# Two heads at a time: preparation of a pair spread over 13 planning rounds in place of 17

## The chip, the cores and the metric

The kernel runs on one core of one Trainium2 chip. The core has five engines that this text names: TensorE (PE, with its weight loads shown apart as PEld), VectorE (DVE), ScalarE (ACT), GpSimd (POOL) and SyncE (SP), which here only starts transfers. Each engine works through its own list of instructions in order and waits on semaphores for the others. The metric is the time of one execution on the device in microseconds, lower is better.

## The reference, cut to what matters

The whole program is three transformer-like blocks over 256 latent tokens and 256 context tokens of width 1024. Only one part of the first block is touched: the recurrent mixer of eight heads, four pairs of heads `p` = 0 to 3, each run in two directions `d` (forward, backward).

```
kk = (k * k_k);  kk = kk / max(sqrt(sum(kk * kk)), 1e-12)
w_raw = w0 + tanh(wl) @ w2[d];   iclr = sigmoid(a0 + al @ a2[d])
decay = exp(-exp(-softplus(-w_raw) - 0.5))
k_dir = k * (1 + (iclr - 1) * k_a)
state = state * w_t + (state @ -kk_t) (kk_t * a_t) + v_t k_t      # 512 steps, per head and direction
y_t   = state @ r_t
```

The steps over time are computed 64 at a time: within a chunk of 64 steps a triangular system is solved with small matrix products, and the chunks are chained afterwards.

## The kernel before, in words

**Stages.** After the projections and the window attention of the first layer (the stage that ends with `step("end", "even")`) comes the stage of the units. A unit is one pair of heads, one direction and one half of the tokens (four chunks of 64), so there are 16 units. `unit` (line 923) gives out its work in 13 rounds: the Gram products (`unit grams`), five levels of the triangular inverse (`unit lt` and `unit tlt`, ten rounds), the solve, and the outputs with the states.

**Preparation.** Before a unit can run, its pair and direction must be prepared. `prepare(p)` (line 811) gives out: squares of the keys, their sums, a clamp and a root, four reciprocals of 128 columns each (`prep recip`, DVE, line 2389) with the product into `kk`, the turned values (`prep v`), and then for each direction two low-rank products (`prep lora`, PE, lines 1915 and 1917, sigmoids on ACT), a scan along time (`prep decay`, DVE, line 2397), exponentials and the gain of the keys (`prep exps`, DVE line 2410, ACT), and products with them (`prep scale`, `prep last`). For pairs 1 to 3 POOL makes these products: in `prep exps` lines 1601 and 1604 or 1606, in `prep scale` lines 1611, 1613 and 1615, in `prep last` lines 1620 and 1622. The last of them, line 1622, tells PE that the direction is prepared; `unit grams` waits for it (line 1852). For pair 0 DVE makes them. POOL also masks each unit's Gram products (lines 3130, 3133, 3136) and makes the mask of one level for each of three `unit lt` steps (line 3136).

**The plan.** The order of the work on every engine comes from one list, `plan`, written by Python generators. `run(...)` asks each generator for one piece in turn; one pass over all of them is called a round here. A `yield` ends what a generator gives out in this round. Each engine later goes through the whole plan in its order and takes out its own part. So a round has no time of its own: it only fixes in what order an engine meets the pieces. In the stage of the units a round asks, in this order: four lanes (each takes the next unit of `work` when it is done with its last, lane n starts 4n rounds later), `preparing`, `chaining` (the chain over the chunks, lines 1933 and 1939 on PE, lines 2448 and 2455 on DVE, and the group norm at the end of a pair with its own reciprocals, line 2466) and `conditions` (32 slices of the modulation product, 16 matmuls of line 1687 each, one in every second round). A lane whose next unit isn't prepared in the plan gives out nothing in that round. The preparation of pair 1 follows on pair 0's; that of pair 2 waits until all units of pair 0 are given out, that of pair 3 for pair 1.

Pair 0 starts earlier, in the stage before, where `begun()` (line 860) asks `prepare(0)` for 11 pieces between projections and attention.

Matmuls of the units all have line 1832 (a helper), copies out of PSUM on ACT line 2727.

Of the kernel before, what the change touches and what calls it, by code (L numbers as in the profile page):

```python
def program(nc, I, C, out):
# [192 lines left out]
    def step(*a):  # L194
        plan.append(a)
# [10 lines left out]
    def take(*key):  # L206
        assert idle, "no bank"
        b, before = idle.pop(0)
        assert key not in uses, key
        uses[key] = Use(b, before)  # L210

    def give(*key):
        u = uses[key]
        idle.append((u.b, u.empty))
# [596 lines left out]
    def prepare(p):  # L811
        step("prep squares", p)
        yield
        take("kk sums", p)
        step("prep sums", p)
        yield
        give("kk sums", p)
        step("prep norm", p)
        yield
        for i in range(4):  # L820
            step("prep recip", p, i)
            if i % 2:
                yield
        for q in range(2):
            take("v turned", p, q)
            step("prep v", p, q)
            give("v turned", p, q)
        yield
        for d in range(2):
            if p or not d:  # L830
                prep_lora(p, d)
                yield
            step("prep decay", p, d)
            yield
            step("prep exps", p, d)
            yield
            step("prep scale", p, d)
            yield
            if not p and not d:
                prep_lora(p, 1)  # L840
                yield
            step("prep last", p, d)
            prepared.add((p, d))
            yield
        step("prep rk", p)
        yield
        take("bonus", p)
        step("prep bonus", p)
        give("bonus", p)

    def prep_lora(p, d):
        take("w", p, d)
        take("a", p, d)
        step("prep lora", p, d)
        give("w", p, d)
        give("a", p, d)

    now = prepare(0)

    def begun():  # L860
        while not projected >= {4, 8, 12, 13}:
            yield
        for _ in range(11):
            next(now)
            yield

    run(a_proj(), b_rotate(), begun(), slowed(modulation(0, 8, 16)))
    step("end", "even")
    top[0] = m_b
# [108 lines left out]
    def preparing(first):  # L978
        yield from first
        for p in range(1, 4):  # L980
            while p > 1 and not all((p - 2, d, h) in finished for d in range(2) for h in range(2)):
                yield
            yield from prepare(p)
# [2367 lines left out]
```

How the kernel before makes its waits and increments, by code:

```python
        def wait_ge(self, sem, value):  # L62
            return self
# [23 lines left out]
        def wait_ge(self, *points):  # L87
            if isinstance(self.e, Stub):
                return
            far = {}
            for p in points:
                if p is not None and p.value > max(self.seen.get(p.of, 0), far.get(p.of, 0)):
                    far[p.of] = p.value
                assert p is None or p.of is not None
            for c, v in far.items():
                self.e.wait_ge(c.h, v)
                self.seen[c] = v
# [1500 lines left out]
    def keys(e, q, p, d):  # L1598
        ka, k = KA[p % 2][d], pA[:, 4 + p, :]
        q.wait_ge(q.last(), at("ka gain", p, d))
        e.tensor_tensor(ka, ka, k, MUL).then_inc(*q.tick())
        q.wait_ge(q.last(), *([at("bonus", p - 1)] if p else []))
        if d == 0:
            e.tensor_copy(kb, ka).then_inc(*q.tick())
        else:
            e.tensor_tensor(kb, kb, ka, ADD).then_inc(*q.tick())
# [1 line left out]
    def scaled(e, q, p, d):  # L1608
        be, ka = BE[p % 2][d], KA[p % 2][d]
        q.wait_ge(q.last(), at("kk", p))
        e.tensor_tensor(be, be, kk, MUL).then_inc(*q.tick())
        q.wait_ge(q.last(), at("falls", p, d))
        e.tensor_tensor(be, be, sg, MUL).then_inc(*q.tick())
        q.wait_ge(q.last())
        e.tensor_tensor(ka, ka, sg, MUL).then_inc(*q.tick(at("scaled", p, d)))
# [1 line left out]
    def rotated(e, q, p, d):  # L1617
        ar = AR[p % 2][d]
        q.wait_ge(q.last(), at("exps", p, d), *(() if p else stage("even")))
        e.tensor_tensor(ar[:, 0, :], cu, kk, MUL).then_inc(*q.tick())
```

## Time and profile before

| | us |
|---|---|
| median of 3 runs | 1977.13 (1973.98 to 1978.09) |
| the profiled execution's own time | 1983.05 |
| its span, first to last instruction | 1981.2 |
| PE busy in the span | 1815.8 |
| stage of the units in the profile | about 245 to 616 |
| PE busy in that stretch | 333.76 of 371.00 |

The span leaves out what lies around the program's own instructions (1983.05 - 1981.2 = 1.85 us). Busy time of PE is the union of its matmuls; weight loads are apart. The mean granted TensorE clock of the execution is 0.958 of full speed.

### The profile page before, as it was taken

The numbers are of one execution on the slowest core, as the hardware profiler recorded it, in microseconds if no ns is written. First come the engines' busy times: TensorE is split into PE (matmuls) and PEld (weight loads), VectorE is DVE, ScalarE is ACT, GpSimd is POOL, SyncE is SP. The second block draws the span as 40 slices with busy tenths as digits, with TensorE's granted clock in tenths as the row PEclk, the third lists the DMA queues.
The fourth block names the chain that finished last, engine by engine and source line by source line (L and its number), as shares of the span: only waits on it lengthen the run. The fifth ranks groups of instructions, "written<-read, shape, count | busy, mean of one in ns | idle before, by whom it ended". The sixth has DMA issues, their size and how long they took to land.

```text
span 1981.2 us, 39345 instructions
## 1 busy us (share of the span) xinstructions
PE 1815.8 (92%) x16690; PEld 1502.1 (76%) x16690; DVE 1103.9 (56%) x1626; ACT 871.7 (44%) x1374; POOL 224.0 (11%) x222
## 2 busy tenths in 40 slices
PE   4999888988898899999998998899989999889997
PEld 2867677877687688888887766798877677769985
DVE  4357654565455744324435866565455475757863
ACT  4136544353332544213325266465332366536643
POOL 0000036334353000000001100000000000000210
PEclk8999989999998999999999999899989999989998
DMA  8341152232222323232324411365545523435542
GB/s 285 112 153 61 55 169 88 94 103 88 87 88 69 124 64 106 85 106 86 107 85 97 148 44 43 108 191 182 190 128 168 191 86 103 150 117 180 191 159 96
DMA packets 201372, 237.13 MB, mean 120 GB/s; under 512 B 14347, under 2 KB 158573, under 8 KB 201197
## 3 DMA queue, kind: packets, MB, share of 16 engines
q1 hardware_dynamic: 196267, 227.52, 35.8%
q10 hardware_dynamic: 4930, 7.11, 1.1%
q8 instruction: 131, 2.15, 0.5%
q14 instruction: 44, 0.36, 0.1%
HBM read 233.56 MB, written 1.05 MB: 118 GB/s over the span
## 4 chain that ended last, share of the span: by engine, by line
PE 74%; DVE 12%; ACT 7%; issue 2%; POOL 2%; DMA 2%; ACTq 0%; SPq 0%; DVEq 0%; POOLq 0%
PE bank L1636 17%; PE bank L1637 17%; PE bank L1638 17%; PE bank L1832 9%; DVE window L2139 3%; ACT window L2727 3%; PE bank L1687 2%; DMA arena<-in_w_ada 2%; PE bank L1820 2%; PE bank L1799 2%; PE bank L1811 1%; PE bank L1839 1%; PE bank L1803 1%; DVE arena L2209 1%; DVE arena L2466 1%
## 5 line engine op out<-in xcount | busy, mean ns | idle before, releaser
L1638 PE MATMUL bank<-window 128*128 128x512 f32 (+1 forms) x1980 | 687.5, 347 | 0.0
L1637 PE MATMUL bank<-window 128*128 128x512 f32 (+1 forms) x1904 | 676.6, 355 | 0.0
L1636 PE MATMUL bank<-window 128*128 128x512 f32 (+1 forms) x1732 | 626.2, 362 | 41.4 <-DVE window L2139 16.5
L1638 PEld LDWEIGHTS bank<-window 128*128 128x128 f32 x1980 | 384.9, 194 | 46.3
L1636 PEld LDWEIGHTS bank<-window 128*128 128x128 f32 x1732 | 338.3, 195 | 101.1 <-DVE window L2139 21.9
L1637 PEld LDWEIGHTS bank<-window 128*128 128x128 f32 x1904 | 371.7, 195 | 46.4 <-issue 0.5
L2139 DVE TENSOR_TENSOR window<-arena,window 128x2048 fp32r<-128x2048 f32 (+1 forms) x132 | 296.6, 2247 | 192.3 <-ACT window L2727 190.7
L2727 ACT ACTIVATE window<-arena 128x2048 fp32r<-128x2048 f32 (+2 forms) x252 | 311.0, 1234 | 183.4 <-DMA arena<-in_w_ff 50.9
L2727 ACT ACTIVATE arena<-bank 128x256 f32<-128x256 f32 (+1 forms) x266 | 115.9, 436 | 352.1 <-PE bank L1638 130.3
L1832 PEld LDWEIGHTS bank<-arena 64*64 64x64 f32 x5888 | 205.0, 139 | 33.8 <-issue 10.3
L1832 PE MATMUL bank<-arena 64*64 64x64 f32 (+1 forms) x5888 | 218.1, 230 | 12.1 <-ACT arena L2727 4.0
L3136 POOL TENSOR_TENSOR arena<-arena 128x256 f32<-128x256 f32 x80 | 68.4, 855 | 331.6 <-DMA arena<-t_id 198.5
L2948 ACT ACTIVATE arena<-bank 128x512 f32<-128x512 f32 (+1 forms) x64 | 31.5, 492 | 146.6 <-PE bank L1638 145.3
L2139 DVE TENSOR_TENSOR window<-arena,window_extra 128x2048 fp32r<-128x2048 f32 (+1 forms) x32 | 71.2, 2226 | 36.7 <-ACT window_extra L2727 36.4
L2356 DVE TENSOR_TENSOR arena<-arena,bank 128x512 f32<-128x512 f32 (+1 forms) x80 | 50.8, 635 | 64.5 <-PE bank L1832 60.7
L1636 PE MATMUL bank<-window,window_extra 128*128 128x256 f32 (+1 forms) x248 | 78.8, 318 | 2.5 <-POOL window L3147 2.5
L2850 ACT ACTIVATE arena<-bank,arena 128x512 f32<-128x512 f32 (+3 forms) x112 | 58.6, 523 | 50.7 <-DVE arena L2300 32.7
L1687 PE MATMUL bank<-arena 128*32 128x256 f32 x768 | 58.7, 424 | 23.0 <-DMA arena<-in_w_ada 20.6
L3178 POOL TENSOR_TENSOR arena<-arena 128x256 f32<-128x256 f32 x22 | 20.0, 911 | 527.6 <-DVE arena L2682 527.0
L1637 PE MATMUL bank<-window,window_extra 128*128 128x256 f32 (+1 forms) x248 | 78.5, 317 | 0.0
L2489 DVE TENSOR_TENSOR arena<-arena 128x512 f32<-128x512 f32 (+1 forms) x48 | 28.9, 603 | 86.2 <-ACT arena L2948 85.6
L1636 PE MATMUL bank<-window_extra,window 128*128 128x512 f32 (+1 forms) x172 | 67.3, 392 | 3.0 <-DVE window L2139 3.0
(298 smaller groups left out, 2028.3 us busy)
## 6 DMA issues: line engine op xcount, KB each, us to landing
arena<-in_w_ff SPq DMA_DIRECT2D x64, 1024.0 KB, 5.4
arena<-in_w_ada SPq DMA_DIRECT2D x48, 1024.0 KB, 6.0
arena<-in_w_in SPq DMA_DIRECT2D x23, 1024.0 KB, 5.1
arena<-in_w_ffn_up SPq DMA_DIRECT2D x22, 1024.0 KB, 5.1
arena<-in_w_ffn_down SPq DMA_DIRECT2D x10, 1024.0 KB, 5.1
arena<-in_w_in_even SPq DMA_DIRECT2D x9, 1024.0 KB, 5.5
arena<-in_w_out SPq DMA_DIRECT2D x8, 1024.0 KB, 5.0
arena<-in_w_in_odd SPq DMA_DIRECT2D x8, 1024.0 KB, 5.5
```

The source lines that it names most:

```text
L1636: e.matmul(o, rr(l[0]), rr(r[0]), start=start, stop=False)
L1637: e.matmul(o, rr(l[0]), rr(r[1]), start=False, stop=False)
L1638: return e.matmul(o, rr(l[1]), rr(r[0]), start=False, stop=stop)
L1687: t = e.matmul(u.b[q:q + 32, 0:256], SV[:, k, 6 - 2 * g:38 - 2 * g], w.v[:, k, :], start=g == 0 and k < 4, stop=g == 3 and k >= 4)
L1799: t = e.matmul(b if it["ns"] > 1 else b[:, 0], it["q"][h0:h1], k, start=True, stop=not it["masks"])
L1820: t = e.matmul(u.b[h0:h1, oc:oc + 128], vs[h], a.PT[i % a.NT][h][0:kw, x * 128:x * 128 + 128], start=it["begin"] and x == 0, stop=it["end" ...
L1832: t = e.matmul(o[h0:h1, c], l[i][h0:h1, c], r[i][h0:h1, c], start=i == 0, stop=i == len(l) - 1)
L2139: e.tensor_tensor(rr(raw), raw, rr(w.high, F32), SUB).then_inc(*ve.tick(w.ready))
L2356: e.tensor_tensor(w, w, x, SUB).then_inc(*ve.tick(b.empty, at("w", *u)))
L2727: return e.activation(o, i, ACT.Copy, **k)
L2850: e.activation(a.P[i % a.NP][h][:, s * n:s * n + n], u.b[:, s * n:s * n + n], ACT.Exp, bias=low[:, x:x + 1], accum_out=total[:, x:x + 1]). ...
L3136: return e.tensor_tensor(z.L[l % 2], z.G[:, :, 0], lvl[:, 1 - d, l:l + 1, :].to_broadcast([128, NCH, 64]), MUL)
```

## The change

The four reciprocals are given out in one round together with the turned values, and after them, in place of two rounds before them. For pairs 1 to 3 the round between `prep scale` and `prep last` goes. `prepare(p)` then has 13 rounds for pairs 1 to 3 and 15 for pair 0, where it had 17 for each. `begun()` asks for 9 pieces in place of 11, so that the pieces of pair 0 in the stage before end at the same step. No instruction is added or removed.

```diff
@@ prepare(p)
         step("prep norm", p)
         yield
-        for i in range(4):
-            step("prep recip", p, i)
-            if i % 2:
-                yield
         for q in range(2):
             take("v turned", p, q)
             step("prep v", p, q)
             give("v turned", p, q)
+        for i in range(4):
+            step("prep recip", p, i)
         yield
...
             step("prep exps", p, d)
             yield
             step("prep scale", p, d)
-            yield
+            if not p:
+                yield
             if not p and not d:
                 prep_lora(p, 1)
                 yield
@@ begun()
-        for _ in range(11):
+        for _ in range(9):
             next(now)
             yield
```

## Rows read from the trace of the kernel before

**Rows 1.** The page, part 1: busy us of each engine, share of the span, instructions.

```profile
PE 1815.8 (92%) x16690; PEld 1502.1 (76%) x16690; DVE 1103.9 (56%) x1626; ACT 871.7 (44%) x1374; POOL 224.0 (11%) x222
```

**Rows 2.** Busy time by stretch, units' stage and before; columns in the first row.

```profile
core 0: us, PE busy (x) PEld busy (x) DVE busy (x) ACT busy (x) POOL busy (x), PEclk, DMA share, GB/s
245.00:616.00 371.00, 333.76 (x8190) 285.13 (x8186) 203.83 (x368) 146.25 (x292) 154.22 (x154) 0.94 0.30 99
...
150.00:245.00 95.00, 88.81 (x626) 62.63 (x626) 70.09 (x163) 58.53 (x128) 0.00 (x0) 0.97 0.15 45
```

**Rows 3.** PE's waits, 245 to 616: waiter, releaser, us in total, times, longest.

```profile
PE bank L1832 <- POOL extra L1622: 12.6, 3, 5.7
PE bank L1933 <- DVE extra L2448: 5.8, 2, 3.6
PE bank L1832 <- ACT arena L2727: 4.0, 4, 1.8
PE bank L1832 <- POOL arena L1622: 3.3, 1, 3.3
...
PE bank L1832 <- DVE arena L2356: 1.8, 1, 1.8
```

**Rows 4.** Line 1687 alone: durations ns (min/median/max), first and last start us.

```profile
L1687 PE MATMUL bank<-arena x512: 377/379/635, 251.9 to 587.6; 128*32 128x256 f32 x171
```

**Rows 5.** POOL in order of time, 300 to 317: start, us, idle before.

```profile
300.09 1.96 POOL L3136 TENSOR_TENSOR arena<-arena 128x256 f32<-128x256 f32 x2 [8.75 <-ACT arena L2727]
302.13 1.52 POOL L3130 TENSOR_TENSOR arena<-arena 128x256 f32<-128x256 f32 x1
303.73 1.59 POOL L3133 TENSOR_TENSOR arena<-arena 128x512 f32<-128x512 f32 x1
305.40 1.93 POOL L3136 TENSOR_TENSOR arena<-arena 128x256 f32<-128x256 f32 x2
307.41 1.28 POOL L1601 TENSOR_TENSOR arena<-arena 128x512 f32<-128x512 f32 x1
...
313.48 0.72 POOL L3136 TENSOR_TENSOR arena<-arena 128x256 f32<-128x256 f32 x1
...
315.62 1.26 POOL L1622 TENSOR_TENSOR extra<-arena 128x512 f32<-128x512 f32 x1
```

**Rows 6.** PE in order of time around the first unit of pair 1.

```profile
300.73 1.07 PE L1687 MATMUL bank<-arena 128*32 128x256 f32 x16
...
305.19 1.61 PE L1832 MATMUL bank<-arena 64*64 64x64 f32 x48 [1.84 <-ACT arena L2727]
...
316.94 2.83 PE L1832 MATMUL bank<-extra 64*64 64x64 f32 x48 [5.24 <-POOL extra L1622]
```

**Rows 7.** Busy time after that stall, columns as in Rows 2.

```profile
315.00:322.00 7.00, 5.06 (x74) 5.06 (x76) 1.39 (x2) 1.19 (x3) 4.10 (x5) 0.52 0.00 0
```

**Rows 8.** POOL for pair 2, first direction: first and last piece.

```profile
415.57 1.09 POOL L1601 TENSOR_TENSOR arena<-arena 128x512 f32<-128x512 f32 x1 [12.66 <-DVE arena L2410]
...
422.27 1.59 POOL L1622 TENSOR_TENSOR arena<-arena 128x512 f32<-128x512 f32 x1
```

**Rows 9.** PE around the first unit of pair 2.

```profile
426.29 0.45 PE L1933 MATMUL bank<-extra,arena 64*64 64x64 f32 x8 [3.56 <-DVE extra L2448]
...
428.21 3.99 PE L1832 MATMUL bank<-arena 64*64 64x64 f32 x74
```

**Rows 10.** POOL for pair 3, second direction: first and last piece.

```profile
547.51 1.27 POOL L1601 TENSOR_TENSOR arena<-arena 128x512 f32<-128x512 f32 x1 [0.66 <-DVE arena L2410]
...
557.22 1.26 POOL L1622 TENSOR_TENSOR extra<-arena 128x512 f32<-128x512 f32 x1
```

**Rows 11.** The reciprocals of the preparation, grouped: busy us, mean ns.

```profile
L2389 DVE RECIPROCAL arena<-arena 128x128 f32<-128x128 f32 x12 | 11.4, 953 | 0.4
```

**Rows 12.** PE where pair 1's second direction is first used.

```profile
348.53 1.57 PE L1832 MATMUL bank<-extra 64*64 64x64 f32 x48
```

**Rows 13.** POOL's last piece for it.

```profile
346.17 1.28 POOL L1622 TENSOR_TENSOR extra<-arena 128x512 f32<-128x512 f32 x1
```

## The prediction

> **What bounds the kernel now.** Start with the busy times of the page [rows 1]: PE works 1815.8 of 1981.2 us, so only its idle time and its clock can give or cost much. The change touches the stage of the units, so the next view is the busy time of that stretch [rows 2]: PE is busy 333.76 of 371.00 us, POOL 154.22, DVE 203.83. 37.24 us of PE's idle time lie here, and the stage can win no more than that, plus what the clock loses with it (mean 0.94). Who ends that idle time stands in PE's waits [rows 3]. The largest share is POOL line 1622, the last product of a preparation: 12.6 us in 3 waits and 3.3 us in one, 15.9 in all. So in four of the six cases of pairs 1 to 3 PE stood at `unit grams` and waited until the direction was prepared. The rest is small: 5.8 us for the chain's DVE step, 4.0 for ACT copies, 1.8 for DVE. The stage is a full PE with holes, and the largest holes are the preparation that comes too late for its first unit.
>
> **What a round is worth.** The 32 slices of line 1687 are in every second round, the first in round 1, and start at 251.9 and about 587 us [rows 4]: 335.5 / 62 = 5.4 us for a round, idle time included. The stage has 70 rounds before (counted below), so PE's work is 333.76 / 70 = 4.8 us in a round.
>
> **Counting the rounds.** From the generators, with round 1 the first of the stage. Before, the pieces `prep last` of (pair, direction) (1,0), (1,1), (2,0), (2,1), (3,0), (3,1) are in rounds 16, 21, 35, 40, 52, 57, and in each case a free lane takes the first unit in the next round. After, they are in rounds 13, 17, 32, 36, 45, 49, and again a lane is waiting or comes free for the next round each time. The last unit ends in round 64 in place of 70. The same work of PE then lies in 64 rounds, 333.76 / 64 = 5.2 us in each. No instruction goes, so PE's busy time doesn't fall: fewer rounds save nothing by themselves. What changes is how much other work PE finds between a step of the preparation and its use.
>
> **The removed round of cover.** POOL's part begins with the gain of the keys in `prep exps` and ends with line 1622. Before, `exps`, `scale`, `last` and the first unit are in rounds R, R+1, R+2, R+3; after, in R, R+1, R+2 with `scale` and `last` together. PE has the rest of round R and one full round less to do meanwhile. Two full rounds of 4.8 us become one of 5.2: 9.6 - 5.2 = 4.4 us of cover go, six times.
>
> POOL's part itself takes 423.86 - 415.57 = 8.3 us when nothing comes between [rows 8] and 558.48 - 547.51 = 11.0 us with level masks between [rows 10]; the six lie in this range. Level masks that the vanished round put between `scale` and `last` (0.72 us for one [rows 5]) now come later; I take 3 us off for them over the six.
>
> Now the six, with the wait or the slack of before. (1,0): 5.24 us wait [rows 6]. (1,1): PE starts at 348.53 and line 1622 ended at 347.45 [rows 12, 13], a slack of 1.1. (2,0): line 1622 ends at 423.86, PE starts the unit at 428.21 [rows 8, 9], slack 4.35. (2,1): 3.3 wait [rows 3]. (3,0) and (3,1): the longest, 5.7, and the remaining 12.6 - 5.24 - 5.7 = 1.7 [rows 3, 6]. With 4.4 us less cover: 9.6, 3.3, 0.05, 7.7, 10.1, 6.1, together 36.9; less the 3 us, 34. Before 15.9. **Term 1: +18 us.**
>
> **A check on (1,0), worked out on its own.** Before, PE's round 13 ends with line 1687 at 300.73 + 1.0 = 301.7 [rows 6], and rounds 14 to 16 cover the preparation until the wait. After, the unit is in round 14, so PE stands at 301.7. POOL starts the Gram masks of the unit of round 13 at 300.09, as ACT lets it, and ends them at 303.73 + 1.59 = 305.3 [rows 5]. The key gains, now a round earlier, fit into its 8.75 us of idle time before that. Then come the five products of `scale` and `last` at 1.34 us each: 305.3 + 6.7 = 312.0. PE waits 10.3 us, against 5.24 + 1.84 before [rows 6]. The mean rule gave 9.6, so it isn't too dark here.
>
> **What is won.** Preparation and lanes move against the chain and the norm. The waits that aren't line 1622's are 5.8 + 4.0 + 1.8 = 11.6 us in PE's list [rows 3]. The ACT wait of 1.84 at 305 falls inside a longer wait; 3.56 at 426 stands where PE waits for a chain step on DVE [rows 9], which in the new plan follows a wait in which DVE catches up; reciprocals of norm and preparation of pair 3 no longer share a round. I take 7 of the 11.6. Bounds: 0 and 11.6. **Term 2: -7 us.**
>
> **Reciprocals together.** Twelve at 0.953 us in the stage [rows 11]: four in one round hold DVE 3.8 us and the product into `kk` follows. A lane's DVE result is used in the lane's next round, 5.2 us on, so the burst hides; only where two lanes stack behind it would it show. Three times at most 3.8 us as the upper bound, 0 as the lower, since no instruction goes. I take 0. The same for pair 0, whose pieces come up to two rounds earlier beside the attention: PE is busy 88.81 of 95.00 us there [rows 2], DVE 70.09. At best it wins 2 of the idle 6.2, at worst one burst of 3.8 shows; I take 0. The stage's transfers are the 32 slices of the modulation, two rounds apart as before, and nothing on SP moves past them.
>
> **Clock.** In the stretch after the wait of 5.24 the granted clock is 0.52 on average over 7 us [rows 7], the lower of the levels 1.2 and 2.4 GHz nearly throughout. PE was partly idle in it, so of 7 us at half speed up to 5.06 us of busy time went at half rate, some 2.5 us lost. Waits that now become long (two more by the list above: (2,1) and (3,1) over 6 us, (1,1) not) can each bring a stretch like it, and those at (1,0) and (3,0) have theirs already. I take 2 us in all, bounds 0 and 5. **Term 3: +2 us.**
> The Trainium skill, TensorE: Matmul & The Clock Gate, section "HAM oscillation — how this bites in real kernels", says that waits between bursts of matmuls throttle the array again and that the loss is half of the time spent throttled. By that rule, an estimate from the page, the stretch of 7 us would cost 3.5 us where the row gives 2.5 and two new ones 7 us in place of 2; the trace shows the throttled stretch after the wait, but not that each long wait brings one.
>
> **Sum.** 18 - 7 + 2 = +13 us. The profiled execution of before took 1983.05 us, 1981.2 in its span, so its like would take 1996; it is 5.9 us over the median of the runs, 1977.13. On the median: 1990.
>
> **Rivals.**
> *Faster: denser rounds cover what the removed round did.* The lanes idle less (rounds 14 to 16 and 18 to 21 before), so between `exps` and the first unit PE may find as much work as before; the reciprocals and pieces of the chain no longer meet on DVE. Then waits on line 1622 stay at 15.9 and most of the 11.6 of the others go, say 9: 1977 - 9 = 1968. For it speaks that slack of 4.35 was unused at (2,0); against it the count at (1,0), where POOL sets the end at 312.0 whatever PE has. It decides from the point where a full round holds over 9 us of PE's work; the mean is 5.2.
> *Nothing: POOL's end moves with the rounds.* The gain of keys stands behind the lanes' DVE steps of its round, and if each is reached 4 us sooner in PE's time because the round before is lighter, terms 1 and 2 cancel: 1977, within 4 us.
> *Heavier: the whole loss shows.* Each case loses a full 5.2 us and the chain's waits stay: 15.9 + 31.2 - 5.45 of slack = 41.7, so +26, nothing won, clock +5: 2008, or 1977 + 28 = 2005 if POOL's 3 us come off.
> *The change doesn't do what it says:* pair 0 still has 15 rounds; that changes nothing in the stage of the units, since its second direction is prepared in round 4 in both plans. It is no case of its own.
>
> **How the numbers follow.** Forecast 0.56, faster 0.20, nothing 0.14, heavier 0.10. A difference of 0.2%, about 4 us, is what a measurement can tell from no change. The forecast's own range is 1982 to 2001. The range down to the faster rival and up to most of the heavier one is 1967 to 2004. Of the forecast some 0.02 lies inside 4 us: slower 0.64, same 0.16, faster 0.20.
>
> **What would show it.** PE's waits between 245 and 616 should have line 1622 at 28 to 40 us in place of 15.9, the one at (1,0) near 10 us and ending at about 312; PE's idle time in the stage near 48 in place of 37; its busy time within 5 us of 334; one more or two more stretches at the lower clock. The wait at DVE line 2448 should be smaller. It is wrong if line 1622's waits stay under 20 us, if busy time moves by more than idle time, or if the difference lies outside the stage.

## The result, and the profile after

The changed kernel takes 1985.01 us (median of 5 runs, 1982.62 to 1987.52) against 1978.07 for the kernel before: a ratio of 1.0034, 95% interval 1.0019 to 1.0049, which is 3.8 to 9.7 us, 6.7 in the middle. The forecast was +13 on the median, 1990, in a range of 1967 to 2004. The direction held and the size came out at half. The two profiled executions differ by less (1983.05 and 1985.01 us), because that of before lies 5 us above the median of its kernel's runs; so here the stages are compared, not the spans.

One line is missing from the changed file ahead of all engines' code, so line 1622 of before is 1621 after, 1687 is 1686, and so on.

First the busy time by stretch (columns as in [rows 2]): from PE's first instruction whose place the change moves to pair 0's first unit, and from there to the last unit. Before:

```profile
145.20:244.60 99.40, 90.39 (x626) 63.52 (x624) 73.62 (x165) 60.39 (x131) 0.00 (x0) 0.96 0.19 59
244.60:614.90 370.30, 333.57 (x8178) 285.07 (x8180) 203.29 (x368) 146.25 (x292) 154.22 (x154) 0.94 0.30 99
```

After:

```profile
144.75:250.20 105.45, 90.78 (x626) 63.78 (x622) 73.61 (x165) 62.83 (x133) 0.00 (x0) 0.95 0.17 55
250.20:618.10 367.90, 330.08 (x8176) 281.81 (x8176) 198.63 (x367) 147.32 (x293) 149.35 (x154) 0.94 0.31 100
```

The stage of the units, where the prediction put the loss, became 2.4 us shorter (370.30 to 367.90). The stretch ahead of it, where the prediction put nothing, became 6.05 us longer (99.40 to 105.45) with the same busy time: PE's idle time there is 9.0 before and 14.7 after.

A second profile of the kernel before (1977.33 us) shows how far one program's profiles differ:

```profile
144.90:243.10 98.20, 89.39 (x624) 62.75 (x624) 72.90 (x163) 60.43 (x131) 0.00 (x0) 0.98 0.19 59
243.10:612.70 369.60, 332.99 (x8150) 285.41 (x8152) 204.27 (x369) 146.00 (x292) 154.03 (x154) 0.95 0.31 99
```

About a microsecond in each stretch. So the +6 ahead of the units is clear of that, and the -2.4 in the units is barely so. A kernel with the change for pairs 1 to 3 alone (below) has the same order in the units and doesn't have the -2.4:

```profile
244.40:615.40 371.00, 331.82 (x8176) 281.89 (x8176) 198.62 (x367) 147.49 (x293) 148.75 (x154) 0.94 0.30 99
```

So no gain of the stage is shown.

PE's waits after, 252 to 640 us (columns as in [rows 3]):

```profile
PE bank L1831 <- POOL extra L1621: 12.1, 4, 9.2
PE bank L1831 <- POOL arena L1621: 10.2, 2, 7.6
...
PE bank L1831 <- ACT arena L2726: 3.2, 4, 1.4
PE bank L1949 <- ACT arena L2936: 2.7, 2, 2.3
```

The last product of the preparation now makes PE wait 22.3 us in six waits, where [rows 3] have 15.9 in four. That is +6.4 us where the prediction had +18; which of the two edits brings it is seen only in the experiments. The first of these waits, for pair 1, in POOL's and PE's order of time:

```profile
300.18 1.28 POOL L1600 TENSOR_TENSOR arena<-arena 128x512 f32<-128x512 f32 x1 [1.33 <-DVE arena L2409]
...
307.13 1.96 POOL L3135 TENSOR_TENSOR arena<-arena 128x256 f32<-128x256 f32 x2 [4.99 <-ACT arena L2726]
...
309.97 1.26 POOL L3132 TENSOR_TENSOR arena<-arena 128x512 f32<-128x512 f32 x1
311.31 1.26 POOL L1610 TENSOR_TENSOR extra<-extra,arena 128x512 f32<-128x512 f32 x1
...
316.66 1.26 POOL L1621 TENSOR_TENSOR extra<-arena 128x512 f32<-128x512 f32 x1
```

```profile
307.76 1.07 PE L1686 MATMUL bank<-arena 128*32 128x256 f32 x16
318.07 2.18 PE L1831 MATMUL bank<-extra 64*64 64x64 f32 x36 [9.23 <-POOL extra L1621]
```

This is the check of the prediction come true: the key gain runs before the Gram masks, five products run behind them without a gap, PE stands idle 9.23 us (10.3 forecast). It ends at 318.07; less the 5.60 us by which the units start later (250.20 against 244.60) that is 312.5, where the prediction had 312.0. PE's waits for the chain's DVE step (line 2448 of before, 5.8 us in [rows 3]) are gone in the stage.

What the stretch ahead of the units lost is seen where the order of PE first changes. Line 1838 is the turning of a pair's values on PE. After:

```profile
144.43 0.70 PE L1798 MATMUL bank<-arena 64*128 64x256 f32 x4
145.96 0.68 PE L1838 MATMUL bank<-arena 64*64 64x64 f32 x16 [0.83 <-ACT arena L2726]
149.51 0.68 PE L1838 MATMUL bank<-arena 64*64 64x64 f32 x16 [2.87 <-DVE arena L2270]
152.56 0.79 PE L1635 MATMUL bank<-window 128*128 128x512 f32 x1 [2.37 <-ACT arena L2849]
```

Before, the turning stood behind two more projections:

```profile
148.43 0.79 PE L1636 MATMUL bank<-window 128*128 128x512 f32 x1 [2.82 <-DVE window L2139]
...
175.17 1.25 PE L1839 MATMUL bank<-arena 64*64 64x64 f32 x32
```

6.07 us of idle time in place of 2.82. The releasers are a copy on ACT, DVE's shift of a projection and ACT's exponentials of the attention. The reciprocals, which the prediction had suspected here, run only later (DVE, after):

```profile
154.81 3.92 DVE L2388 RECIPROCAL arena<-arena 128x128 f32<-128x128 f32 x4
```

### The profile page after: what moved, and what is told of

It is laid out like the page before. It is cut to its first block, busy times and chain, and to the rows that moved or that the text cites. A ratio compares the mean times of both kernels' runs of the same rounds, so it can differ in the third digit from the quotient of the medians.

```text
span 1983.2 us, 39337 instructions
## 1 busy us (share of the span) xinstructions
PE 1813.9 (91%) x16690; PEld 1500.7 (76%) x16690; DVE 1100.4 (55%) x1626; ACT 874.7 (44%) x1377; POOL 218.9 (11%) x222
## 4 chain that ended last, share of the span: by engine, by line
PE 74%; DVE 11%; ACT 7%; POOL 3%; issue 2%; DMA 2%; SPq 0%; ACTq 0%; DVEq 0%; POOLq 0%
PE bank L1635 18%; PE bank L1636 17%; PE bank L1637 17%; PE bank L1831 9%; DVE window L2138 3%; ACT window L2726 3%; PE bank L1819 2%; PE bank L1686 2%; DMA arena<-in_w_ada 2%; PE bank L1798 2%; PE bank L1810 1%; PE bank L1838 1%; PE bank L1802 1%; PE bank L2016 1%; DVE arena L2208 1%
## 5 line engine op out<-in xcount | busy, mean ns | idle before, releaser
L1831 PEld LDWEIGHTS bank<-arena 64*64 64x64 f32 x5888 | 203.9, 139 | 38.6 <-issue 11.1
L1831 PE MATMUL bank<-arena 64*64 64x64 f32 (+1 forms) x5888 | 216.5, 229 | 17.9 <-POOL arena L1621 10.2
```

Of the source, the lines that this page charges most:

```text
L1831: t = e.matmul(o[h0:h1, c], l[i][h0:h1, c], r[i][h0:h1, c], start=i == 0, stop=i == len(l) - 1)
```

## The experiments

Every ratio is to the kernel before, measured beside it. Waits on the last product of the preparation (line 1622 of before), by pair and direction, read from PE's order of time in each trace, in us:

| kernel | (1,0) | (1,1) | (2,0) | (2,1) | (3,0) | (3,1) | sum |
|---|---|---|---|---|---|---|---|
| before | 5.2 | 0 | 0 | 3.3 | 5.7 | 1.7 | 16.0 |
| changed | 9.2 | 0.8 | 2.6 | 7.7 | 1.2 | 0.9 | 22.4 |
| reciprocals together | 9.3 | 3.4 | 0 | 1.1 | 1.3 | 6.7 | 21.7 |
| scale and last together | 6.9 | 5.2 | 5.2 | 4.4 | 9.9 | 7.4 | 38.9 |
| by pair | 5.2 | 0 | 0 | 1.1 | 3.0 | 0 | 9.3 |

**Pair 0's part alone.** `prepare(0)` and `begun()` as in the change, pairs 1 to 3 as before.

```diff
+        for i in range(4 if p else 0):
             step("prep recip", p, i)
...
+        for i in range(0 if p else 4):
+            step("prep recip", p, i)
...
-        for _ in range(11):
+        for _ in range(9):
```

> Of the change only pair 0's part: its four reciprocals in one round after the turned values, its pieces two rounds earlier beside the attention; pairs 1 to 3 as before. Theory of the trace (the loss sits in the stage before the units, where PE's idle time rose from 9.0 to 14.7 us in the changed kernel): +5 to +6 us, and the stretch from PE's first different instruction to pair 0's first unit near 105 us in place of 99.4. Rival, the prediction's: pair 0's part costs nothing, 0 us within 2.

1.0038 (1.0026 to 1.0051), +7.5 us. PE's idle time ahead of the units is 14.7 us, the waits of the units stage those of before to 0.1 us. Pair 0's part carries the whole loss; that it costs nothing has fallen.

**Pairs 1 to 3 alone.** Reciprocals together and the round between `scale` and `last` gone for `p` over 0; pair 0 as before.

> Only the part of pairs 1 to 3 (13 rounds each); pair 0 as before with 17. Theory of the trace (the stage of the units became 2 to 3 us shorter although line 1622's waits rose from 16.0 to 22.4 us): -3 to +1 us. Rival, the prediction's: the removed round of cover sets the sum, +7 to +13 us.

1.0001 (0.9990 to 1.0013). The waits are those of the changed kernel. The forecast for these pairs was +13, so its part of the sum fails here. The two halves add up: 7.5 + 0.2 against 6.7 measured, within the intervals.

**Reciprocals together, pairs 1 to 3.**

```diff
-        for i in range(4):
+        for i in range(4 if not p else 0):
...
+        for i in range(0 if not p else 4):
+            step("prep recip", p, i)
```

> For pairs 1 to 3 only the reciprocals in one round (15 rounds for each); scale and last keep their round between them; pair 0 as before. Prediction's view: preparation starts its later pieces two rounds sooner against the lanes, the cover between exps and the first unit stays, so line 1622's waits stay at 16 us or fall, the time falls by 2 to 6 us. Rival: a burst of 3.8 us on DVE delays the lanes: up to +4 us, with new waits of PE on DVE line 2356.

0.9977 (0.9965 to 0.9989), -4.5 us. The waits on the last product rose to 21.7 and yet the time fell, so the first expectation had the time right and the waits wrong. No new wait on DVE shows: line 2356's counterpart holds PE 0.6 us.

This kernel keeps the round between `scale` and `last`, and still has 21.7 us of waits where before has 16.0 and the changed kernel 22.4. So most of the change's +6.4 comes with the reciprocals, not with the removed round. At (1,0) PE has more work in front of the unit than before (10.3 us from the end of the key gain, 5.0 before) and waits longer, because POOL's products now stand behind another unit's masks:

```profile
294.14 1.28 POOL L1603 TENSOR_TENSOR arena<-arena 128x512 f32<-128x512 f32 x1 [1.34 <-DVE arena L2412]
...
301.09 1.96 POOL L3138 TENSOR_TENSOR arena<-arena 128x256 f32<-128x256 f32 x2 [5.00 <-ACT arena L2729]
...
305.28 1.26 POOL L1613 TENSOR_TENSOR extra<-extra,arena 128x512 f32<-128x512 f32 x1
...
312.24 1.26 POOL L1624 TENSOR_TENSOR extra<-arena 128x512 f32<-128x512 f32 x1
```

From the end of the key gain (294.00) to the last product POOL needs 19.5 us, and 10.1 before.

**Scale and last together, pairs 1 to 3.**

```diff
             step("prep scale", p, d)
-            yield
+            if not p:
+                yield
```

> For pairs 1 to 3 only the round between scale and last removed (15 rounds for each); reciprocals and pair 0 as before. Prediction's view: one round of cover less in each of six cases, line 1622's waits rise from 16 to over 28 us, time +8 to +13 us. Rival (the count by average rounds was too coarse; what PE finds in the rounds that are left decides): waits rise by under 8 us and others fall, -2 to +3 us.

1.0110 (1.0093 to 1.0127), +22 us. By itself this edit does what the prediction gave the whole change, and more. Its waits in the trace:

```profile
PE bank L1833 <- POOL extra L1623: 29.3, 4, 9.9
PE bank L1833 <- POOL arena L1623: 9.6, 2, 5.2
```

and the stage of the units:

```profile
243.20:638.00 394.80, 337.43 (x8178) 289.69 (x8180) 200.18 (x368) 146.22 (x292) 151.14 (x154) 0.92 0.29 93
```

38.9 us of waits. Of the 24.5 us by which the stage grew, 20.6 are idle time and 3.9 the same work at a lower mean clock (0.92). The longest wait is that of pair 3's first direction. PE around it:

```profile
524.80 0.61 PE L1695 MATMUL bank<-arena 128*128 128x8 f32 x4
525.35 1.15 PE L1833 MATMUL bank<-arena 64*64 64x64 f32 x32
526.42 1.07 PE L1688 MATMUL bank<-arena 128*32 128x256 f32 x16
537.40 2.83 PE L1833 MATMUL bank<-extra 64*64 64x64 f32 x48 [9.91 <-POOL extra L1623]
```

By the count of the generators two lanes stand still in the last round ahead of the unit, waiting for the preparation of pair 3 (one for each direction), and PE finds 1.1 us of lane work and a slice. In the changed kernel the same round holds a full set:

```profile
508.13 3.89 PE L1831 MATMUL bank<-arena 64*64 64x128 f32 x112
511.85 0.63 PE L1838 MATMUL bank<-arena 64*64 64x64 f32 x16
512.32 2.03 PE L1831 MATMUL bank<-arena 64*64 64x64 f32 x64
514.19 0.63 PE L1838 MATMUL bank<-arena 64*64 64x64 f32 x16
514.75 1.07 PE L1686 MATMUL bank<-arena 128*32 128x256 f32 x16
517.00 1.61 PE L1831 MATMUL bank<-extra 64*64 64x64 f32 x48 [1.18 <-POOL extra L1621]
```

Both this kernel and the one with the reciprocals together end in round 66 by the count of the generators, and they are 26 us apart: the number of rounds says nothing of the time.

**Pair 0: where it costs.** Two kernels, a slip in both: their expectations say that pairs 1 to 3 are as before, but the reciprocals were together in all pairs. Their yardstick is therefore the kernel with the reciprocals together, 0.9977.

The first keeps the early turned values with the burst and puts two rounds behind them; the second puts all of pair 0's preparation two rounds later:

```diff
             step("prep recip", p, i)
         yield
+        if not p:
+            yield
+            yield
```

```diff
     def prepare(p):
+        if not p:
+            yield
+            yield
```

> Pair 0's four reciprocals together in their old round after the root, then two empty rounds, so that its low-rank products and all that follows stand where they stood before; pairs 1 to 3 as before. Theory A (the burst of 3.8 us on DVE, in front of the attention's reductions of that round, makes PE wait): the loss of pair 0's part stays, +4 to +8 us. Theory B (the two rounds by which everything after moves against attention and projections make it): 0 us within 2.

> Pair 0's preparation with four reciprocals together but begun two rounds later, so that its squares and the burst come two rounds later than before and the rest stands where it stood; pairs 1 to 3 as before. Theory A (burst): some loss stays wherever it meets attention, +2 to +8 us. Theory B (position of the later pieces): 0 us within 2.

0.9984 (0.9974 to 0.9995) and 0.9973 (0.9961 to 0.9986). Against the yardstick that is +1.4 us and -0.8, neither told from nothing. The traces are finer: the first has the waits of 0.83, 2.86 and 2.37 us at the turned values again, 11.8 us idle ahead of the units, where the second, whose turned values are back at 175 us, has 9.5, and the yardstick 9.8. So the early round with turned values and burst comes with 2 to 3 us of idle time, the whole preparation begun two rounds later with nothing. No run moved the turned values alone; that it is they and not the burst is read from who waits.

**One round earlier, no burst.**

```diff
-            if i % 2:
+            if i % 2 and (p or i < 3):
...
-        for _ in range(11):
+        for _ in range(10):
```

> Pair 0 with its reciprocals two and two as before, but the turned values in the round of the second two, so that its low-rank products and all later pieces come one round earlier beside the attention; pairs 1 to 3 as before. Theory B (the position of the later pieces costs): +2 to +5 us for one round. Theory A (the burst of four costs): 0 us within 2, since no round has more than two reciprocals.

0.9993 (0.9981 to 1.0005). One round costs nothing, against theory B as it was priced. PE's idle time ahead of the units is even 7.5 us here, 1.5 less than before; but at the first slice of the stage it then waits 4.5 us for its weights (2.8 before). So the loss comes only with two rounds; no run has the two rounds without the burst. Of the 5.7 us of idle time more in the changed kernel, 3.3 are the three waits where the turned values meet the projection (6.07 against 2.82), and 2.4 come later, where all other pieces meet other rounds of the attention: 6.6 us in place of 4.2, on ACT's exponentials, copies and DVE's shift. That the second part comes from the place of the later pieces is read from the trace only, and the 7.5 us of time (5.1 to 10.1) are known less well than the 5.7 us of idle time.

**Last product early, units where they were.**

```diff
             step("prep scale", p, d)
+            if p:
+                step("prep last", p, d)
             yield
...
-            step("prep last", p, d)
+            if not p:
+                step("prep last", p, d)
```

> For pairs 1 to 3 the products of last come with those of scale as in the kernel that lost 21 us, but the direction counts as prepared in the plan one round later, so that every unit and every other piece stands where it stood before. Theory (the loss was cover: the first unit's products stood one round too early in PE's list): -2 to +1 us, waits at 12 to 16 us. Rival (it is the order of POOL's work, five products without a gap in front of the level masks): +5 us or more, with PE waiting for copies and masks.

0.9993 (0.9982 to 1.0004), waits 14.3 us. The same order of POOL's five products as in the kernel that lost 22 us, and nothing lost: what cost was the place of the unit, and of all that moved up with it, in PE's list, not that POOL makes the five products in a row.

**By pair.** Pairs 0 and 1 with 17 rounds, pair 2 with reciprocals together (15), pair 3 with both (13), pairs 1 to 3 each chosen where the table has the smallest waits.

```diff
-        for i in range(4):
+        for i in range(4 if p < 2 else 0):
...
+        for i in range(0 if p < 2 else 4):
+            step("prep recip", p, i)
...
             step("prep scale", p, d)
-            yield
+            if p < 3:
+                yield
```

> Structure by pair: pairs 0 and 1 with 17 rounds as before, pair 2 with reciprocals together (15), pair 3 with reciprocals and scale with last together (13). Theory of counted cover (a wait is what POOL needs after the key gain, 8 to 11 us, less the PE work that the plan puts before the first unit): waits on the last product of the preparation 5 to 9 us in all where they were 16.0, time -6 to -12 us. Rival (the cover of one pair depends on shifts that the other pairs bring, no rule holds): anywhere within 4 us of the kernel with reciprocals together, -4.5.

0.9918 (0.9902 to 0.9935), 1962.51 us, -16 us: more than expected. Its waits and its stage of the units:

```profile
PE bank L1835 <- POOL extra L1625: 8.2, 2, 5.2
PE bank L1690 <- DMA arena<-in_w_ada: 5.1, 1, 5.1
```

```profile
242.60:598.30 355.70, 325.80 (x8178) 277.31 (x8178) 205.66 (x367) 147.50 (x293) 152.47 (x154) 0.97 0.32 103
```

14.6 us shorter than before, 6.8 of them idle time (36.7 to 29.9), 7.8 the same matmuls in less busy time at a mean granted clock of 0.97 in place of 0.94. By the count it ends in round 64, like the changed kernel. The wait of 5.1 us for the weights of the stage's first slice (2.8 before) is nearly as long as the longest one for the preparation; no run went after it. This is the fastest version found.

**By pair, with pair 0 as in the change.**

> The structure by pair of the fastest kernel so far (pair 1 with 17 rounds, pair 2 with 15, pair 3 with 13), and pair 0 as in the change (reciprocals together, all later pieces two rounds earlier beside the attention). If the loss of pair 0's part belongs to the attention stage alone and adds to the rest: +5 to +9 us over the kernel by pair, so -10 to -6 against before, with PE's idle time before pair 0's first unit 5 to 6 us above. Rival (it cost 7.5 us only through what it shifted in the stage of the units): within 2 us of the kernel by pair, -15.

0.9970 (0.9957 to 0.9982), 10 us slower than by pair, just over the +5 to +9 expected. PE's idle time ahead of the units is 14.7 us again, 9.1 by pair. So pair 0's part adds to the rest: 10 us here against 7.5 alone, which the intervals don't tell apart.

**By pair, pair 1's first unit a round later.**

```diff
             step("prep last", p, d)
+            if (p, d) == (1, 0):
+                yield
             prepared.add((p, d))
```

> The kernel by pair with one empty round before pair 1's first direction counts as prepared. Theory of cover: its wait of 5.2 us goes to 0 to 1 us, as another round of lane work stands in front of it, and the time falls by 2 to 5 us against the kernel by pair. Rival (the empty round moves pair 1's second direction and its lanes, and another wait takes its place): within 1.5 us of it or slower.

0.9940 (0.9925 to 0.9954), slower than by pair by about 4 us: the stage of the units is 3.7 us longer, 1.2 of it idle time and 2.5 the same matmuls busy for longer. The wait of 5.2 us is gone, as the theory says, and the rival is right about the time: pair 1's second direction now waits 5.19 us, because POOL takes another unit's Gram masks between its products:

```profile
342.77 1.26 POOL L3138 TENSOR_TENSOR arena<-arena 128x512 f32<-128x512 f32 x1
344.11 1.26 POOL L1625 TENSOR_TENSOR extra<-arena 128x512 f32<-128x512 f32 x1
```

**The kernel before, again.**

> The kernel before, unchanged, profiled a second time: how far two profiles of one program differ in their stages. Both theories: waits on the last product of the preparation 16.0 us within 0.5, PE's idle time before the first unit 9 us within 1.5; the stretch at the lower clock at the start of the stage of the units may differ.

1977.33 us, idle 8.8 us ahead of the units, waits 14.4 us (3.7 at (1,0) in place of 5.2: the expected 16.0 within 0.5 missed), the rest within 0.1.

## Why the prediction came out as it did

The time lies in the range, but that is luck for the most part: the part that was to cost 13 us cost 0.2, and a part priced at nothing cost 7.5. Two of the prediction's own signs of being wrong came true: the difference lies outside the stage of the units, and inside it busy time moved by more (-3.5 us) than idle time (+1.1). The waits on line 1622, at 22.3 us, lie between its bounds of 20 and 28, and PE's idle time in the stage is 37.8 us, not near 48.

**Term 1, the removed round of cover: +18 forecast, +6.4 found.** A wait here is the difference of two stretches that both start at the end of the key gain: what POOL needs until the last product, less the cover, which is the time until PE reaches the first unit in its list (its work and its other waits). The step as put, "Two full rounds of 4.8 us become one of 5.2", is right for the edit it describes. The cover in the six cases was 5.0, 11.4, 12.8, 7.1, 3.1 and 9.5 us before; with only that edit it is 2.5, 5.3, 3.4, 6.1, -1.0 and 4.9, a mean loss of 4.6 us against 4.4 forecast, and 38.9 us of waits against 36.9. But the change has a second edit, and the list of six was made as if it had not. With the reciprocals together the later pieces come two rounds earlier against the lanes, and in all cases but (2,1) more of the lanes' work falls into the gap than with the removed round alone: 8.8, 10.3, 5.6, 2.8, 7.8 and 9.5 us. POOL's need isn't fixed either: 8.4 to 11.1 us before, but 17.9 at (1,0) of the changed kernel, and 19.5 and 15.3 at (1,0) and (3,1) with the reciprocals together, because masks of other units, and what POOL waits for ahead of them, come between. The one case worked out from its own rounds, (1,0), came out right (10.3 against 9.2), and by the need, not by less cover; pair 3's two, taken by the mean, were forecast at 10.1 and 6.1 and are 1.2 and 0.9. The count of the generators was there to do all six.

**Reciprocals together: 0 forecast, -4.5 us found**, 3.9 of them in the stage of the units. No DVE burst showed, as said. What was overlooked is that a step without a price moves everything behind it. On top of the reciprocals together the removed round costs 4.7 us (0.9977 to 1.0001), without them 22 (1.0000 to 1.0110). The edits don't add, so none could have been priced alone.

**Pair 0: 0 forecast, +7.5 found**, over the upper bound of 3.8. The text priced the burst of reciprocals and forgot the turned values that moved with them; their matmuls stand in PE's list and wait for what DVE and ACT have yet to do for the projection. This term stands in for what the units didn't lose, so the total came into the range for the wrong reason.

**Term 2, other waits: -7 forecast.** PE's idle time in the units apart from line 1622 went from 20.7 to 15.4 us, -5.3, and to 16.8 with pairs 1 to 3 alone. The 5.8 us for the chain's DVE step and the wait of 1.84 at (1,0) fell away as argued, but waits of the group norm's variance product (line 1949) for ACT's squares, 2.7 us, are new. The prediction's 11.6 us for all waits that aren't line 1622's was too little: the same list has another 9 us, 2.8 for a transfer, 2.1 for DVE line 2379 and 3.6 for no releaser among them.

**Term 3, the clock: +2 forecast, -3.5 in this pair of profiles.** The mean granted clock of the stage is 0.94 before and after, and PE's busy time went from 333.57 to 330.08 us. Two profiles of one program differ here too: from 252 to 262 us the granted clock is 0.59 in the first profile of before and 1.00 in the second, so a difference of this size isn't put down to the change. The term's idea holds over the set. In the 7 us behind the wait of 5.73 us of before the granted clock is 0.63, behind the one of 9.91 with scale and last together 0.64, behind the one of 7.65 of the changed kernel 0.65, where full speed is 2.4 GHz and the lower level 1.2; and the same 8178 matmuls are busy 337.4 us with 38.9 us of waits and 325.8 with 9.3. The Trainium skill, TensorE: Matmul & The Clock Gate, section "HAM oscillation — how this bites in real kernels", has half of the throttled time lost. By that rule the step from a mean clock of 0.94 (before) to 0.97 (by pair) in 370 us is 0.03 x 370 = 11 us, an estimate. The trace has 7.8 us of busy time less; as the two clocks are rounded to hundredths, which is up to 3.7 us of the 11, it neither confirms nor contradicts the rule.

**The rivals.** The faster one said that denser rounds cover what the removed round did. For pair 3 it was right, and its objection, that a full round would need over 9 us, compared a mean with the one round that mattered: the changed kernel's round ahead of (3,0) holds 7.7 us of PE's work (508.13 to 514.75 + 1.07), that of the kernel with scale and last together alone 2.1 (525.35 to 526.42 + 1.07).

## What to carry to other kernels

Where engines take their work from one planned list, removing a pause changes who stands in front of whom, and what it costs is read from the work that the plan puts between the last producer and the first consumer in that very place, case by case, and from what stands between the producer's own pieces; a mean per round hid covers from -1.0 to 12.8 us and needs from 8.1 to 19.5. Price every step that moves, the matmuls too, not only the one that the change is about. And try a rule by part: the removed round cost 22 us for three pairs alike, while in pair 3, with the reciprocals together, the waits with it are smaller (1.2 and 0.9 us against 1.3 and 6.7), and the kernel that has it there only is the fastest; no run has pair 3's removed round alone.

## What the runs showed of the hardware

The clock weighed more than expected. Between the slowest and the fastest kernel of the set (394.80 and 355.70 us for the units) 27.5 us are idle time of PE and 11.6 us are the same matmuls taking longer, at mean granted clocks of 0.92 and 0.97. That is some 0.4 us through the clock for each microsecond of waits, between these two. It is no fixed price: the kernel by pair with pair 0 as in the change has less idle time in the units than by pair (27.1 against 29.9 us) and yet the same matmuls are busy 3.6 us longer (329.35 against 325.80), at a mean granted clock of 0.95 in place of 0.97.
